# The second layer's experts with the token slots stationary and the weights moving, in three one-pass products

## The reference, cut to what matters

```python
N_EXPERTS = 16
EXPERT_FF = 512
...
    top_aff, idx = lax.top_k(jnp.swapaxes(aff, 1, 2), cap)
    xg = jax.vmap(lambda hb, ib: hb[ib])(h, idx)
    hid = jax.nn.silu(jnp.einsum('becd,edf->becf', xg, w_gate)) * jnp.einsum('becd,edf->becf', xg, w_up)
    y = jnp.einsum('becf,efd->becd', hid, w_down) * top_aff[..., None].astype(h.dtype)
    return jax.vmap(lambda yb, ib: jnp.zeros((n_tok, d), yb.dtype).at[ib.reshape(-1)].add(yb.reshape(-1, d)))(y, idx)
```

## Time and profile before

| | us |
|---|---|
| median of 3 runs | 5588.57 |
| lowest, highest | 5584.09, 5598.72 |
| the profiled execution | 5588.13 |
| its span | 5586.3 |
| second layer's expert stage, first load to next stage's first load | 3123.62 to 3506.64 |

### The profile page before, as it was taken

How to read it: one execution, slowest core, us unless ns; L and a number is a source line. 1 busy time by engine, 2 the same in 40 slices (tenths; PEclk the granted TensorE clock), 3 DMA queues, 4 the chain that set the end, 5 groups by cost and what they waited for, 6 DMA issues and landing times. The chain is left out here.

```text
span 5586.3 us, 56594 instructions
## 1 busy us (share of the span) xinstructions
PE 4770.9 (85%) x22000; PEld 3404.4 (61%) x22000; DVE 2344.2 (42%) x3729; ACT 1086.9 (19%) x1999; POOL 483.6 (9%) x623
## 2 busy tenths in 40 slices
PE   8878989889899969697997599796777499998996
PEld 2765658674666647474876488585544278884453
DVE  0336768735000041577873300424433745551023
ACT  1103323320111021132332011201122221110021
POOL 0200000100111220100010011100011100000001
PEclk9987889898899989799997799897665699999997
DMA  6110000114656521000011587120000111111101
GB/s 267 64 38 1 1 16 1 50 59 179 247 211 217 188 92 72 23 1 17 1 57 42 230 333 275 60 79 24 5 0 1 41 72 47 48 46 75 41 34 42
DMA packets 70644, 460.62 MB, mean 82 GB/s; under 512 B 9376, under 2 KB 13360, under 8 KB 53296
## 3 DMA queue, kind: packets, MB, share of 16 engines
q1 hardware_dynamic: 57360, 410.76, 19.1%
q0 software_dynamic: 13088, 47.19, 3.3%
HBM read 397.11 MB, written 60.82 MB: 82 GB/s over the span
## 5 line engine op out<-in xcount | busy, mean ns | idle before, releaser
L1737 PEld LDWEIGHTS psum<-words,words 128*128 128x128 f32 x4096 | 514.7, 192 | 21.7 <-issue 21.7
L1737 PE MATMUL psum<-words,words 128*128 128x160 f32 (+1 forms) x4096 | 518.8, 289 | 1.4 <-DVE words L417 0.9
L824 PE MATMUL psum<-words,words 128*128 128x512 f32 (+1 forms) x1080 | 408.9, 379 | 95.5 <-DVE words L540 46.3
L1051 PEld LDWEIGHTS psum<-words 128*128 128x128 f32 x2928 | 403.9, 199 | 100.9 <-issue 84.5
L697 PE MATMUL psum<-words,words 128*128 128x512 f32 x1104 | 438.4, 397 | 24.4 <-DVE words L735 20.2
L185 PE MATMUL psum<-words 128*128 128x512 f32 (+3 forms) x896 | 389.0, 596 | 65.4 <-DMA words<-in_w_down 23.1
L698 PE MATMUL psum<-words,words 128*128 128x512 f32 x1104 | 439.7, 398 | 0.0
L699 PE MATMUL psum<-words,words 128*128 128x512 f32 x1104 | 431.7, 391 | 0.0
L1051 PE MATMUL psum<-words 128*128 128x128 f32 x2928 | 429.2, 284 | 0.4 <-DVE words L1173 0.4
L825 PE MATMUL psum<-words,words 128*128 128x512 f32 (+1 forms) x1080 | 404.3, 374 | 0.0
L826 PE MATMUL psum<-words,words 128*128 128x512 f32 (+1 forms) x1080 | 403.4, 374 | 0.0
(11 more groups left out here) (314 smaller groups left out, 6786.3 us busy)
## 6 DMA issues: line engine op xcount, KB each, us to landing
words<-in_w_gate SPq DMA_DIRECT2D x32, 2048.0 KB, 7.8
words<-in_w_up SPq DMA_DIRECT2D x32, 2048.0 KB, 12.3
words<-in_w_down SPq DMA_DIRECT2D x32, 2048.0 KB, 11.1
words<-in_ada_w SPq DMA_DIRECT2D x24, 2048.0 KB, 7.8
words<-in_w_in SPq DMA_DIRECT2D x55, 512.0 KB, 3.2
words<-in_w_up SPq DMA_DIRECT2D x44, 512.0 KB, 3.2
words<-in_w_down SPq DMA_DIRECT2D x8, 1408.0 KB, 6.1
parked<-words SPq DMA_DIRECT2D x2, 5120.0 KB, 17.5
```

What stands on the lines that cost most here:

```text
L824: pe.matmul(out, hi[:, j, w], x[0](kt, t0, n), start=(kt == 0), stop=False)
L1051: mm = pe.matmul(obanks[s % O][:, 0:P], values, pt[:, s % 2, t, :], start=(t == 0), stop=(t == nt - 1))
L1737: mm = pe.matmul(k.bank[m % 2][:, u * W:(u + 1) * W], ring[:, j, w0:w0 + P], xgT[:, j, kt, 0:W], start=(kt == 0), stop=(kt == KD - 1))
```

## The change

The second layer gets its own function, `experts_by_slot`; the first layer keeps `experts`. Nothing else is changed.

- For gate and up, the turned tokens are stationary and the weights move: 8 steps of 128 input features, two banks (gate, up), three `fp32r` products each, 48 products of 128 x 512 in all. The slots come out as rows, so silu and the multiply are one 128 x 512 instruction each, and the hidden values are turned back by 4 more transposes.
- The weights of gate and up come in four pieces for each expert (256 input features of both, two transfers of 512 KB, rows of 4 KiB), into a ring of `RAW` = 7 pieces. ACT rounds each piece to its high part (two instructions of 128 x 1024, ring `SPLIT` = 3) and DVE writes the rest (two of 128 x 1024). Tokens are split the same way.
- `w_down` still comes as one 2 MiB transfer, double buffered, with the plain 32-bit product, but it stands in SP's queue behind the third piece of the next expert.
- PE's order is: products of e, transposes of e+1, results of e-1, transposes of the hidden values of e.
- POOL runs the same small operations and transfers as before. It starts with two gathers ahead of its loop in place of one, so the gather behind the scatter of e is for e+3, and the results of e are made on PE one expert later than before.

```diff
--- before.py
+++ after.py
@@ -1815,6 +1815,232 @@
             pairs(dve, body)
 
 
+def experts_by_slot(k, l):
+
+
+    U, RAW, SPLIT = 4, 7, 3
+    W = 2 * 1024
...
+    with k.stage() as (block, sem):
...
+        @block.sync
+        def _(sp):
+            def results_weights(e):
+                if e >= 2:
+                    sp.wait_ge(d_used, e - 1)
+                sp.dma_start(down[:, e % 2, :], k.a["w_down"][l * NE + e]).then_inc(w_d[e % 2], 16)
+
+            for e in range(NE):
+                for u in range(U):
+                    n = U * e + u
+                    if n >= RAW:
+                        sp.wait_ge(w_used, n - RAW + 1)
+                    sp.dma_start(raw[:, n % RAW, 0:1024], k.a["w_gate"][l * NE + e][:, 1024 * u:1024 * u + 1024]).then_inc(w_in[n % RAW], 16)
+                    sp.dma_start(raw[:, n % RAW, 1024:2048], k.a["w_up"][l * NE + e][:, 1024 * u:1024 * u + 1024]).then_inc(w_in[n % RAW], 16)
+                    if e and u == 2:
+                        results_weights(e - 1)
+            results_weights(NE - 1)
+
+        @block.gpsimd
+        def _(pool):
...
+            def gather(e):
+                if e >= 2:
+                    pool.wait_ge(x_full, 2 * (e - 1))
+                hold(pool)
+                pool.tensor_copy(lslot[e % 2], rl[:, e:e + 1]).then_inc(idx_set, 1)
+                pool.wait_ge(idx_set, e + 1)
+                hold(pool)
+                pool.indirect_dma_start(xg[:, e % 2, :], None, k.rows, bass.IndirectOffsetOnAxis(ap=lslot[e % 2], axis=0)).then_inc(g_in[e % 2], 16)
+
+            gather(0)
+            gather(1)
+            for e in range(NE):
+                if e + 2 < NE:
+                    gather(e + 2)
+                pool.wait_ge(y_out, 2 * (e + 1))
+                if e:
+                    pool.wait_ge(s_done, 16 * e)
+                hold(pool)
+                pool.tensor_copy(lout, rl[:, e:e + 1]).then_inc(out_idx, 1)
+                pool.wait_ge(out_idx, e + 1)
+                hold(pool)
+                pool.indirect_dma_start(acc, bass.IndirectOffsetOnAxis(ap=lout, axis=0), ys[:, e % 2, :], None,
+                                        compute_op=ALU.add).then_inc(s_done, 16)
+            pool.wait_ge(s_done, 16 * NE)
+
+        @block.tensor
+        def _(pe):
+            def tokens(e):
+                pe.wait_ge(g_in[e % 2], 16 * (e // 2) + 16)
+                for q in range(2):
+                    if e:
+                        pe.wait_ge(x_lo, 2 * (e - 1) + q + 1)
+                    for f in range(4):
+                        c0 = (4 * q + f) * P
+                        mm = pe.transpose(k.bank[2 + q][:, f * P:(f + 1) * P], xg[:, e % 2, c0:c0 + P], k.ident[:, :])
+                    mm.then_inc(x_full, 1)
+
+            def turned(e):
+                pe.wait_ge(hid_in, e + 1)
+                if e:
+                    pe.wait_ge(h_out, e)
+                for f in range(4):
+                    mm = pe.transpose(k.bank[4][:, f * P:(f + 1) * P], hid[:, f * P:(f + 1) * P], k.ident[:, :])
+                mm.then_inc(h_full, 1)
+
+            def products(e):
+                for u in range(U):
+                    n = U * e + u
+                    pe.wait_ge(w_lo, 2 * n + 2)
+                    if u % 2 == 0:
+                        pe.wait_ge(x_lo, 2 * e + u // 2 + 1)
+                    if u == 0 and e:
+                        pe.wait_ge(hid_in, e)
+                    for kt in range(2 * u, 2 * u + 2):
+                        x = slice(kt * P, (kt + 1) * P)
+                        for b in range(2):
+                            w = slice(1024 * b + 512 * (kt % 2), 1024 * b + 512 * (kt % 2) + 512)
+                            pe.matmul(k.bank[b][:, :], xhi[:, e % 2, x], whi[:, n % SPLIT, w], start=(kt == 0), stop=False)
+                            pe.matmul(k.bank[b][:, :], xhi[:, e % 2, x], wlo[:, n % RAW, w], start=False, stop=False)
+                            mm = pe.matmul(k.bank[b][:, :], xlo[:, e % 2, x], whi[:, n % SPLIT, w], start=False, stop=(kt == KD - 1))
+                            if u == U - 1 and kt == KD - 1 and b == 0:
+                                mm.then_inc(gu_full, 1)
+                    mm.then_inc(w_used, 1)
+
+            def results(e):
+                pe.wait_ge(w_d[e % 2], 16 * (e // 2) + 16)
+                pe.wait_ge(h_out, e + 1)
+                for h in range(2):
+                    if e:
+                        pe.wait_ge(y_out, 2 * (e - 1) + h + 1)
+                    for kt in range(4):
+                        w0 = kt * D + h * 512
+                        mm = pe.matmul(k.bank[5 + h][:, :], hidT[:, e % 2, kt * P:(kt + 1) * P], down[:, e % 2, w0:w0 + 512],
+                                       start=(kt == 0), stop=(kt == 3))
+                    mm.then_inc(y_full, 1) if h == 0 else mm.then_inc(d_used, 1)
+
+            tokens(0)
+            for e in range(NE):
+                products(e)
+                if e + 1 < NE:
+                    tokens(e + 1)
+                if e:
+                    results(e - 1)
+                turned(e)
+            results(NE - 1)
+
+        def take_tokens(act, e):
+            for q in range(2):
+                act.wait_ge(x_full, 2 * e + q + 1)
+                if e >= 2 and q == 0:
+                    act.wait_ge(w_used, U * (e - 1))
+                act.activation(xhi[:, e % 2, 512 * q:512 * q + 512], k.bank[2 + q][:, :], ACT.Copy).then_inc(x_hi, 1)
+
+        def rest_of_tokens(dve, e):
+            for q in range(2):
+                dve.wait_ge(x_hi, 2 * e + q + 1)
+                dve.tensor_tensor(xlo[:, e % 2, 512 * q:512 * q + 512], k.bank[2 + q][:, :],
+                                  xhi[:, e % 2, 512 * q:512 * q + 512].bitcast(F32), ALU.subtract).then_inc(x_lo, 1)
+
+        @block.scalar
+        def _(act):
+            def split(n):
+                act.wait_ge(w_in[n % RAW], 32 * (n // RAW) + 32)
+                if n >= SPLIT:
+                    act.wait_ge(w_used, n - SPLIT + 1)
+                for b in range(2):
+                    act.activation(whi[:, n % SPLIT, 1024 * b:1024 * b + 1024], raw[:, n % RAW, 1024 * b:1024 * b + 1024],
+                                   ACT.Copy).then_inc(w_hi, 1)
+
+            def scaled(e):
+                if e >= 2:
+                    act.wait_ge(s_done, 16 * (e - 1))
+                for h in range(2):
+                    act.wait_ge(y_full, e + 1) if h == 0 else act.wait_ge(d_used, e + 1)
+                    act.activation(ys[:, e % 2, 512 * h:512 * h + 512], k.bank[5 + h][:, :], ACT.Copy,
+                                   scale=al[:, e:e + 1]).then_inc(y_out, 1)
+
+            split(0)
+            take_tokens(act, 0)
+            split(1)
+            split(2)
+            for e in range(NE):
+                split(U * e + 3)
+                if e + 1 < NE:
+                    split(U * e + 4)
+                act.wait_ge(gu_full, e + 1)
+                act.activation(sg, k.bank[0][:, :], ACT.Silu).then_inc(silu, 1)
+                if e + 1 < NE:
+                    take_tokens(act, e + 1)
+                    split(U * e + 5)
+                if e:
+                    scaled(e - 1)
+                act.wait_ge(h_full, e + 1)
+                act.activation(hidT[:, e % 2, :], k.bank[4][:, :], ACT.Copy).then_inc(h_out, 1)
+                if e + 1 < NE:
+                    split(U * e + 6)
+            scaled(NE - 1)
+
+        @block.vector
+        def _(dve):
+            def split(n):
+                for b in range(2):
+                    w = slice(1024 * b, 1024 * b + 1024)
+                    dve.wait_ge(w_hi, 2 * n + b + 1)
+                    dve.tensor_tensor(wlo[:, n % RAW, w], raw[:, n % RAW, w], whi[:, n % SPLIT, w].bitcast(F32),
+                                      ALU.subtract).then_inc(w_lo, 1)
+
+            split(0)
+            rest_of_tokens(dve, 0)
+            split(1)
+            split(2)
+            for e in range(NE):
+                split(U * e + 3)
+                if e + 1 < NE:
+                    split(U * e + 4)
+                dve.wait_ge(silu, e + 1)
+                dve.wait_ge(w_used, U * (e + 1))
+                dve.tensor_tensor(hid, sg, k.bank[1][:, :], ALU.mult).then_inc(hid_in, 1)
+                if e + 1 < NE:
+                    rest_of_tokens(dve, e + 1)
+                    split(U * e + 5)
+                    split(U * e + 6)
+
+
 def combine(k, l, with_ctx):
 
     XT = k.at(XT0, KD, NT)
@@ -1839,7 +2065,10 @@
     XT, HT = k.at(XT0, KD, NT), k.at(HT0, KD, NT)
     norm(k, XT, HT, KD, ALL if with_ctx else LAT, gain, lambda kt, t0: mod(k, l, 3, kt, t0))
     route(k, l, with_ctx)
-    experts(k, l, with_ctx)
+    if with_ctx:
+        experts(k, l, with_ctx)
+    else:
+        experts_by_slot(k, l)
     combine(k, l, with_ctx)
 
 
```

30 lines of the change are left out of this document (added).

## The result

The changed kernel is slower. Its median is 5619.31 us (5614.74 to 5625.12, 5 runs), that of the kernel before, run beside it, 5596.31 us (5584.09 to 5598.72); the ratio is 1.0048, with a 95% interval of 1.0034 to 1.0063. The profiled execution took 5619.31 us. The forecast was 5558, so it was wrong in sign.

The account below looks back on a forecast made before the run. PE bounds the kernel at 22.23 us an expert, the gather loop close behind. Gain 18.5 - 3.6 - 3 + 13 x (22.23 - 20.8), 30 us, takes 5588.1 to 5558 us; range 5539 to 5583.

Parts of the forecast that it names:

- PE's work: PE's busy time per expert after the change: products 11.16, transposes 0.93 and 0.47, results 6.97; 19.5 us, before 22.23.
- the splits hidden: ACT's and DVE's splitting of weights and tokens, 12.6 and 12.0 us an expert, fits beside PE's work and costs nothing.
- the gather loop: Transposes, results, scatter, gather, landing, next transposes: 12.37 + 8.4 = 20.8 us an expert, becoming the bound; chance 0.47.
- The formula for the gain: Whole stage: start gain 18.5, end loss 3.6, slow clock and first waits 3, plus 13 x (22.23 - T).
- T: Time of one expert in the stage's steady part, from transposes to next transposes: 22.23 us before, 20.8 forecast.
- A: Part of an expert from the start of its transposes to the scatter's issue; forecast at 9.97 us.
- B: Part of an expert from the scatter's issue to the start of the next transposes; forecast at 10.8 us.
- Between 7.3 and 9.7 I take 8.4, the middle.: Gather's landing after its issue: 9.7 us before, 8.4 forecast, as 4 KiB rows would hold it up less.
- The 12.37 us stay.: Time from an expert's transposes to the gather's issue is unchanged, POOL's list and the order of results being the same.
- rival 3: DVE's two-input instructions hold up POOL's preparation of the gather: one to two waits of 1.241 us an expert; chance 0.19.
- Such small holes have not cost the clock.: PE's waits of about 1.3 us ahead of the transposes leave its clock up; an earlier stretch still had 0.96.
- Rival 4: Deep weight queue starves the gathers: landing 13.7 us, 26.1 us an expert, costing 38 us; decides from 12.1; chance 0.09.

Follow-up runs that it names:

- e4: Changed kernel with `w_down` of each expert loaded as four 512 KB transfers with 4 KB rows instead of one; 5624.16 us, ratio 1.0054 to the kernel before.
- e10: Changed kernel with one piece of gate and up weights loaded and read by every split, the other pieces left out; 5569.84 us, ratio 0.9950.
- e3: Changed kernel with scatter and gather reading indices directly from the list of rows, without the copy and one hold; 5615.89 us, ratio 1.0030.
- e2: Changed kernel with twelve products of constants into an unused bank ahead of PE's wait for the gather; 5599.81 us, ratio 1.0000.
- e8: Changed kernel with `w_down` one piece later in SP's order, so issued behind the scatter; 5663.66 us, ratio 1.0117.
- e9: Changed kernel with `w_down` loaded only for the first two experts and used again for the others; 5648.89 us, ratio 1.0100.

## Why the prediction was wrong

Right: PE's work (19.5 forecast, 19.11 measured where nothing waits), the splits hidden, POOL's packets (4.0 us an expert forecast; 16.2% of 317 us for 13 experts is 4.0), and that the gather loop becomes the bound. The formula for the gain holds as well: 300.9 - 13 x 24.51 is a loss of 17.7 us, and the stage lost 20.0 (the third transposes came at 39.9 us in place of 37). What was wrong is T, 24.51 for 20.8. By the loop, A was forecast at 12.37 - 2.40 = 9.97 and came out at 11.13, and B at 2.40 + 8.4 = 10.8 and came out at 13.15. These 3.5 us are the error, and 0.2 more lie in a few longer intervals.

1. **"Between 7.3 and 9.7 I take 8.4, the middle."** This is the step that failed first; alone it takes away most of the gain, and with the next two the sign turns. From the scatter's issue to the gather's landing it took 2.40 + 9.7 = 12.1 us before, and I forecast 10.8 on the ground that short rows would hold a gather up less. Measured is 13.1 (B, to the start of the next transposes, is 13.15). Kept at 12.1, T would have been 22.07 and the gain 14 us, within the bound of no change. The wait behind the queued weights stayed as it was (4.8 us before, 4.9 after), and shorter rows of `w_down` did not shorten it (5.4 in e4). What grew is the passing of POOL's packets, 6.9 to 7.7 us. In the kernel before, SP issued nothing while the gather passed; with the ring of seven pieces it issues 1 MB every 2.7 us, and these pieces share the engines just then. e10 prices them: 2.1 us of B. The landing itself (8.8) looks near 8.4 only because the gather is issued 1.95 us later behind the scatter, while the scatter waits: that is luck. It is no constant, as e3 shows, and the loop should have been measured from the scatter. The first layer's 7.3 to 7.8 that the choice leaned on were the least and the median of the earlier trace rows, which also has 16.5.

2. **"The 12.37 us stay."** They became 11.13 + 4.35 = 15.5, 3.1 more. Of this, 1.95 is POOL beside DVE's products, the mechanism of rival 3: the copy took 1.19 us and the hold behind it 1.06, where it had been 0.79 and 0.19. Its rule in the Trainium skill ("SBUF — State Buffer", section Who interferes with whom) agrees with the stretching. The price that rival 3 put on it does not come: e3 took the copies away, and B stayed. The other 1.16 is in A: 1.62 for the clock, less 0.46 by which A is shorter than forecast when the clock stays up (9.51).

3. **"Such small holes have not cost the clock."** For the hole that was forecast, 1.3 us, this holds: behind the holes of 0.9 to 1.6 us in e10 the granted clock stayed at 1.00. But it is no ground for the hole that came, 3.3 us each expert, and that one brings 0.50 behind it; the row cited the earlier trace rows was of a window with many short gaps. e2 prices it: 1.62 us in A, 16 us in the stage. It follows from the first step, and makes it dearer.

4. **Rival 4** came nearest, with the weight queue beside the gathers, at 0.09. It required landings of 12.1 us, which did not come (8.8), and it put the fault on the depth of the queue, which no run varied. I judged each part alone and found each small; but they come together, and feed one another: a later gather makes a hole, the hole halves the clock, and the slower results make the next scatter later.

## What to carry to other kernels

When work on the bound engine is shortened, measure the next loop from its first transfer to the last landing, with everything that stands in the same queue, and ask what the other queue will be issuing at that moment. If a gather's input doesn't depend on the results, issue it ahead of the wait for them, or at least ahead of the scatter: here the exchange turned 0.48% slower into 0.8% faster, and one expert earlier made it 0.9%. A wait on TensorE can cost more than its length if work on the loop stands right behind it: here 3.3 us of it brought 1.6 us more.

## What the runs showed of the hardware

- Of two queues with work, in these traces the one whose transfers were issued earlier was served first and for long: POOL's first packets came 4.9 us after issue with `w_down` ahead (4.8 in the kernel before), and 2.2 us after issue with nothing ahead (e8, e9). In e8 and e9 the scatter kept the later piece waiting. Once both run, they alternate roughly by packet (123 to 116 in the change, 77 to 83 in e8), with packets of 4 KB and of 16 KB alike.
- A scatter-add's packet holds an engine longer than a load's of the same size: 123 packets (0.50 MB) took 63.3% of 16 engines for 4 us, the pieces' 116 (0.48 MB) 32.2%.
- Fewer bytes can be slower: without `w_down` (e9, 208 GB/s in place of 309 in the steady part) the stage grew by 22 us.
- The granted clock fell to 0.50 behind each single hole of about 3.3 us and stayed at 1.00 behind holes of 0.9 to 1.6 (e10).
